# A hybrid decoder layer on one core: bias rows by the GpSimd queue, down weights as 32 KB rows, block turns by VectorE

## The chip, the cores and the metric

The kernel runs on one core of one Trainium2 chip. The metric is the device time of one launch in microseconds (us), lower is better; each number is a median over several executions.

## The reference

One inference step of one decoder layer in float32, D = 2048, for 256 prompt tokens and 8 sample tokens (one new token each for 8 sequences with a 2048-long cache). Cut to what matters:

```python
z = rms(x) @ w_in                         # 2048 x 3584: [q | k | v | u]
# 12 heads x 64: three dilated windows (128,1) (512,4) (2048,16), merged by softmax denominators,
# QK-norm, T5 relative-position bias rel_bias[bucket(distance)]
# u: 4 groups x 320 channels: causal mean over 2/4/8/16 minus the token, per-group map, scale
x = x + concat(attn, pooled) @ w_out
# cross attention, 4 heads x 128, into 256 memory tokens (prompt) or cached memory (samples)
mk, mv = rms(rms(mem) @ w_ck), rms(mem) @ w_cv
x = x + cross(rms(x) @ w_cq, mk, mv) @ w_co
# mixture of experts: top 1 of 4 groups, top 2 of its 8 experts
for e in range(32):
    y += gate * ((silu(h_e @ w_e_gate[e]) * (h_e @ w_e_up[e])) @ w_e_down[e])     # 2048x512, 2048x512, 512x2048
```

Outputs are also the new caches: the 8 sequences' key and value windows shifted by one row (about 100 MB read and written from DRAM to DRAM), the pooled state, the memory's keys and values.

## The kernel before

The program is written by hand, one instruction stream for each engine (`block.sync`, `block.gpsimd`, `block.tensor`, `block.scalar`, `block.vector`), with semaphores between them; nothing is reordered. Prompt and sample tokens are worked on together, 264 columns. Weights come through `ring`, three 4 MB slots. Slots 0 and 1 take the weight pieces of the front in turn: `CK`, `CV`, seven pieces of w_in (`IN0` to `IN0+6`), pool_w, four of w_out, `CQ`, `CO`. `big(i)` on SyncE's queue (SP) loads piece i and first waits (`piece_used`) until TensorE has used piece i-2, so each load starts at a point of TensorE's program and must land by a later one. ScalarE issues the 64 parts of the DRAM-to-DRAM cache copy (`cache_part`, 1.5 MB each) at fixed points of its own program. GpSimd's queue (POOL) loads constants, then key rows, value rows and memory rows of the samples.

PSUM is two rings of four banks: `vbank` (emptied by VectorE, order in `V_ORDER`) and `abank` (emptied by ScalarE, `A_ORDER`).

The order of TensorE's work in the front: turn the memory rows; project to memory keys (`memory_keys`); turn the x rows (16 times two 128x128 turns and a small one, L693 to L699); two small bias products and one for the row scales (L700 to L712); memory values with `CV` (L714 to L716); turn memory keys; w_in in five pieces for q, k, v (`project`, L726); in piece 1 the bias is spread: SP stores the 12 bias rows (`brow`) to DRAM, loads them back as a Hankel block, and TensorE multiplies it by a flip matrix in six products (L732 to L736) that VectorE negates into `bias`. Then ten `channels` (u) interleaved with attention scores, sample values, pool maps, `sel` (which picks each sample's own heads, L889 to L893), w_out in 16 column tiles (L895 to L913), the cross queries with `CQ`. VectorE scales the rows of `CQ` in place in four parts after the whole piece has landed (L1793 to L1797), and TensorE waits for all four (L915).

The mixture of experts: the tokens of an expert are taken in blocks of 32 (`BLK`). For each block i TensorE gathers the rows by a one-hot product (`gather`, into bank pb[0], 32 rows x 4 column quarters on the 128 partitions), ScalarE copies them out (`rows_out`), TensorE turns them (`turn_rows`), VectorE scales them by the norm gains into `XT` (`rows_in`). `expert(i)` multiplies `XT` by gate and up weights in two halves (16 rows of 512 per partition, 8 a half), ScalarE takes exp, VectorE forms `hid`, TensorE turns it, ScalarE copies it to `aT`, TensorE multiplies by the down weights, and `combine` adds the block to the tokens (VectorE, `add_results`).

On SP, `expert_weights(i)` waits for each half of expert i-1 to be used and loads the next half (2 MB of gate and 2 MB of up), then waits for the down slot and loads 4 MB:

```python
sp.dma_start(slot2.rearrange("p (k n) -> p k n", k=4), src.rearrange("(k p) n -> p k n", p=P))   # L504: 8 KB runs
```

Experts 0 and 1 are special: half 0 of expert 0 and both their down weights are loaded during the cross attention and its output; half 1 of expert 0 when `CO` has been used; the quarters of expert 1 when TensorE has used a quarter (`first_quarter`, L1153) or a half of expert 0 (L527 to L530). Before expert 0 TensorE runs filler products (`keep_busy`), the gather, and, after VectorE's `weights_of_pairs` and `blocks_over`, one small product for blocks that overflow (L1189) whose result `slots_over` turns into `over_done`, which expert 0 waits for.

Of the kernel before, what the change touches and what calls it, by code (L numbers as in the profile page):

```python
# [15 lines left out]
P = 128  # L16
# [4 lines left out]
NB = 8  # L21
# [21 lines left out]
NBUCKET, MAXD = 32, 2048  # L43
BRANCHES = ((128, 1), (512, 4), (2048, 16))
# [41 lines left out]
CONST_W = dict(ident=P, tri=P, moe=NE + NE + 3 + OVB + BLK, corr=NCORR, pools=PG * NB, flip=P, hmask=VC, sel=VG * NB,  # L86
# [9 lines left out]
def constants():  # L96
# [8 lines left out]
    part("flip")[:] = np.eye(P)[::-1]  # L105
# [26 lines left out]
V_ORDER = (["mem"] * 8 + ["gains"] + ["ck"] + ["bias"] * 2 + ["scale"] + ["cv", "in", "in"] + ["flip"] * 6 + ["in"] * 3  # L132
           + ["score"] * 12 + ["sscore"] * 2 + ["state", "svals"] + ["out"] * KT + ["cq"] * 3 + ["xscore"] * 2 + ["cq"] + ["xscore"] * 2
           + ["xsscore", "ssum", "logits", "pos"])
A_ORDER = (["ck"] + ["x"] * 16 + ["cv"] + ["mk"] * 2 + ["in", "sin"] * 5
# [12 lines left out]
def hybrid_decoder_layer(nc, a):  # L148
    with ExitStack() as ctx:
# [6 lines left out]
        bias_dram = nc.dram_tensor("bias_rows", (H, 384), F32, kind="Internal").ap()  # L156
# [41 lines left out]
        bias_flat = slot2[:, 4608:4608 + H * SEQ]  # L198
        biasS = slot2[:, 7680:7680 + NDEC]
        flip = slot2[:, 8192 - P:8192]  # L200
        hankel = qkm[:, 0:H * SEQ]
# [88 lines left out]
        XT = xfree[:, 2112:2624].rearrange("p (j s) -> p j s", j=4)  # L290
# [21 lines left out]
        w_landed = [sem("w_landed0"), sem("w_landed1")]  # L312
        v_filled, v_freed = sem("v_filled"), sem("v_freed")
# [33 lines left out]
        pick_ready, xe_filled, xe_ready = sem("pick_ready"), sem("xe_filled"), sem("xe_ready")  # L347
# [5 lines left out]
        xt_filled, xt_ready = sem("xt_filled"), sem("xt_ready")  # L353
        gate_exp, hid_seq, hid_ready = sem("gate_exp"), sem("hid_seq"), sem("hid_ready")
        hidT_filled, hidT_ready = sem("hidT_filled"), sem("hidT_ready")
# [15 lines left out]
        def piece_landed(eng, i):  # L371
            assert i != CK
            eng.wait_ge(w_landed[i % 2], 16 * (i // 2 + i % 2))
# [7 lines left out]
        N_FIRST, N_CONST = 6, 18  # L381
# [3 lines left out]
        def piece_used(eng, i):  # L385

            if i in (CK, CV):
                eng.wait_ge(v_filled, v_at(("ck", "cv")[i]))
# [22 lines left out]
        def _(sp):  # L411
            def big(i):
# [16 lines left out]
                sp.dma_start(dst, src).then_inc(w_landed[i % 2], 16)  # L429
# [10 lines left out]
            for w, lo, n in (("w_rg", 0, NG), ("w_re", NG, NE)):  # L440
# [8 lines left out]
            sp.dma_start(hankel.rearrange("p (h j) -> p h j", h=H),  # L449
                         bass.AP(tensor=bias_dram.tensor, offset=0, ap=[[1, P], [384, H], [1, SEQ]]))\  # L450
                .then_inc(bias_landed, 16)
# [65 lines left out]
            w1 = a["w_e_down"][0][1].rearrange("(k p) n -> p k n", p=P)  # L517
# [21 lines left out]
            w = a["w_e_down"][0][NE - 1].rearrange("(k p) n -> p k n", p=P)  # L539
# [22 lines left out]
        def _(pool):  # L562
# [24 lines left out]
            for dst, src in ((rb[0:NBUCKET], a["rel_bias"]), (ohp[0:33], cc("ohp", 33)), (ohs[0:33], cc("ohs", 33)),  # L587
                             (tri[:], cc("tri")), (flip, cc("flip")), (moec[:], cc("moe")), (corr[:], cc("corr")),
# [9 lines left out]
            pool.dma_start(gE[:], a["norm_ffn_g"][0].rearrange("(p k) -> p k", k=KT)).then_inc(const_landed, 16)  # L598
            pool.wait_ge(pads_ready, 1)
# [33 lines left out]
        def _(pe):  # L633
# [59 lines left out]
            for t in range(3):  # L693
                pe.wait_ge(x_landed[t], 16)
            for k in range(KT):
                bk = abank("x")
                for t in range(2):
                    turn(bk[:, P * t:P * t + P], xraw[:, t, P * k:P * k + P], ident[:])
                turn(bk[:, SEQ:TOK], xraw[0:NB, 2, P * k:P * k + P], ident[0:NB, 0:NB]).then_inc(a_filled, 1)  # L699
# [13 lines left out]

            piece_landed(pe, CV)  # L714
            project(hmT, wk(CV), 0, abank("cv"), a_filled)
# [10 lines left out]
            for n in range(5):  # L726
# [162 lines left out]
            pe.wait_ge(v_freed, v_at("svals"))  # L889
            bk = abank("sel")  # L890
            for i in range(2):
                last = mm(bk[:, 24 * i:24 * i + 24], masked[0:96, P * i:P * i + P], sel[0:96, :], start=True, stop=True)
            last.then_inc(a_filled, 1)  # L893

            for o in range(KT):  # L895
# [171 lines left out]
            all_emptied()  # L1067
# [3 lines left out]
            def gather(i):  # L1071

                pe.wait_ge(pick_ready, i + 1)
                if not (isinstance(i, int) and i == 0):
                    pe.wait_ge(xt_ready, i)
                for t in range(3):
                    n = P if t < 2 else NB
                    for c in range(4):
# [3 lines left out]

# [1031 lines left out]
```

## Time and profile before

| what | value |
|---|---|
| median of 3 runs | 1549.89 us (1549.2 to 1556.62) |
| profiled execution, its own time | 1553.96 us |
| its span (first to last instruction) | 1552.1 us |
| TensorE busy in the span | 1255.0 us, 81% |
| VectorE, ScalarE, GpSimd busy | 500.3, 194.7, 59.6 us |
| moved by the DMA engines | 608.85 MB, mean 392 GB/s |

A profile's busy time of matrix products is modelled. "PEclk" is the TensorE clock that was granted, as a share of full speed: 1.00 is 2.4 GHz, 0.50 is 1.2 GHz. "DMA share" is the mean busy share of the core's 16 DMA engines; it can read a few per cent over 1 because packets overlap. L660 is line 660 of the kernel.

### The profile page before, as it was taken

The numbers are of one execution on the slowest core, as the hardware profiler recorded it, in microseconds if no ns is written. First come the engines' busy times: TensorE is split into PE (matmuls) and PEld (weight loads), VectorE is DVE, ScalarE is ACT, GpSimd is POOL, SyncE is SP. The second block draws the span as 40 slices with busy tenths as digits, with TensorE's granted clock in tenths as the row PEclk, the third lists the DMA queues.
The fourth block names the chain that finished last, engine by engine and source line by source line (L and its number), as shares of the span: only waits on it lengthen the run. The fifth ranks groups of instructions, "written<-read, shape, count | busy, mean of one in ns | idle before, by whom it ended". The sixth has DMA issues, their size and how long they took to land.

```text
span 1552.1 us, 23601 instructions
## 1 busy us (share of the span) xinstructions
PE 1255.0 (81%) x10109; PEld 654.6 (42%) x10109; DVE 500.3 (32%) x1043; ACT 194.7 (13%) x466; POOL 59.6 (4%) x111
## 2 busy tenths in 40 slices
PE   7999999998998999877776766766776776776676
PEld 4444467765877766322222222222222222222222
DVE  2301155740103224333323323323323323332333
ACT  3200113311111233000000000000000000000000
POOL 2000022221000000000000000000000000000000
PEclk9999999999999999898989988988999899898998
DMA  9999999999999998899999999999999999999997
GB/s 352 312 375 365 356 327 391 359 319 388 383 392 350 316 409 291 336 424 425 427 427 424 429 427 423 428 427 425 427 427 425 427 427 425 426 427 426 424 428 292
DMA packets 114606, 608.85 MB, mean 392 GB/s; under 512 B 11262, under 2 KB 14485, under 8 KB 79849
## 3 DMA queue, kind: packets, MB, share of 16 engines
q1 hardware_dynamic: 72603, 479.04, 74.9%
q10 hardware_dynamic: 34550, 100.80, 17.8%
q0 software_dynamic: 7408, 28.37, 5.1%
q8 instruction: 34, 0.56, 0.1%
q14 instruction: 11, 0.09, 0.0%
HBM read 603.16 MB, written 106.18 MB: 457 GB/s over the span
## 4 chain that ended last, share of the span: by engine, by line
DMA 52%; PE 44%; DVE 2%; issue 1%; SPq 1%; ACT 0%; DVEq 0%; ACTq 0%
DMA ring<-in_w_e_up_dram 45%; PE pb L1150 11%; PE pb L660 9%; PE pb L905 6%; PE pb L746 4%; DMA ring<-in_w_out_dram 2%; DMA ring<-in_w_in_dram 2%; DMA ring<-in_w_cq_dram 2%; PE pb L1032 2%; PE pb L923 2%; PE pb L688 2%; PE pb L666 1%; SPq L490 1%; PE pb L1182 1%; PE pb L1012 1%
## 5 line engine op out<-in xcount | busy, mean ns | idle before, releaser
L1150 PE MATMUL pb<-ring,xT 128*32 128x256 f32 x4096 | 312.6, 472 | 194.0 <-DMA ring<-in_w_e_up_dram 191.5
L1150 PEld LDWEIGHTS pb<-ring,xT 128*32 128x32 f32 x4096 | 154.8, 134 | 374.9 <-DMA ring<-in_w_e_up_dram 236.1
L2033 DVE TENSOR_TENSOR Z<-pb,Z 128x512 f32<-128x512 f32 x248 | 153.7, 683 | 357.9 <-PE pb L1103 357.9
L660 PE MATMUL pb<-ring,hreg 128*128 128x512 f32 (+1 forms) x320 | 125.3, 551 | 0.0
L1182 PE MATMUL pb<-ring,xT 128*32 128x512 f32 x960 | 110.9, 603 | 0.0
L1103 PE MATMUL pb<-xT 32*128 32x512 f32 x744 | 102.9, 623 | 0.0
L1079 PE MATMUL pb<-Z,xT 128*32 128x512 f32 (+1 forms) x768 | 94.9, 608 | 0.0
L660 PEld LDWEIGHTS pb<-ring,hreg 128*128 128x128 f32 x320 | 60.3, 190 | 61.8 <-issue 60.2
L905 PE MATMUL pb<-hreg,ring 128*128 128x264 f32 x320 | 78.0, 401 | 4.7 <-DMA ring<-in_w_out_dram 4.7
L746 PE MATMUL pb<-hreg,ring 128*128 128x264 f32 x320 | 75.3, 395 | 2.1 <-DMA ring<-in_w_in_dram 2.1
L1522 ACT ACTIVATE xT<-pb 128x128 f32<-128x128 f32 x32 | 8.9, 277 | 523.0 <-PE pb L1150 523.0
L905 PEld LDWEIGHTS pb<-hreg,ring 128*128 128x128 f32 x320 | 62.2, 199 | 15.7 <-DMA ring<-in_w_out_dram 5.2
L746 PEld LDWEIGHTS pb<-hreg,ring 128*128 128x128 f32 x320 | 61.2, 193 | 14.5 <-DMA ring<-in_w_in_dram 2.5
L2030 DVE TENSOR_TENSOR Z<-pb,Z 128x512 f32<-128x512 f32 x31 | 21.4, 692 | 98.9 <-PE pb L1103 98.9
L1182 PEld LDWEIGHTS pb<-ring,xT 128*32 128x32 f32 x960 | 28.5, 111 | 55.8 <-issue 55.2
L2057 DVE TENSOR_SCALAR xT<-xT 128x128 f32<-128x128 f32 x32 | 7.3, 227 | 137.3 <-ACT xT L1522 137.3
L905 PE MATMUL pb<-Z,ring 128*128 128x264 f32 x192 | 45.3, 386 | 0.0
L1160 PE MATMUL pb<-ident,xT 128*128 128x128 f32 x32 | 10.5, 329 | 39.9 <-DVE xT L2063 39.9
L1786 DVE TENSOR_TENSOR xT<-pb,xT 128x264 f32<-128x264 f32 x16 | 6.9, 432 | 104.7 <-PE pb L905 104.7
L1087 PE MATMUL pb<-ident,xT 128*128 128x128 f32 x128 | 20.1, 280 | 25.3 <-ACT xT L1513 25.3
L1079 PEld LDWEIGHTS pb<-Z,xT 128*32 128x32 f32 (+1 forms) x768 | 18.4, 108 | 51.3 <-issue 47.5
L905 PEld LDWEIGHTS pb<-Z,ring 128*128 128x128 f32 x192 | 36.5, 190 | 6.2
(337 smaller groups left out, 1135.8 us busy)
## 6 DMA issues: line engine op xcount, KB each, us to landing
ring<-in_w_e_gate_dram SPq DMA_DIRECT2D x61, 2048.0 KB, 19.0
ring<-in_w_e_up_dram SPq DMA_DIRECT2D x61, 2048.0 KB, 23.5
ring<-in_w_e_down_dram SPq DMA_DIRECT2D x30, 4096.0 KB, 22.0
out_win_k_sample_dram<-in_cache_win_k_dram ACTq DMA_DIRECT2D x24, 1536.0 KB, 14.1
out_win_v_sample_dram<-in_cache_win_v_dram ACTq DMA_DIRECT2D x24, 1536.0 KB, 15.1
ring<-in_w_in_dram SPq DMA_DIRECT2D x7, 4096.0 KB, 29.2
ring<-in_w_out_dram SPq DMA_DIRECT2D x4, 4096.0 KB, 34.3
out_win_k_sample_dram<-in_cache_win_k_dram ACTq DMA_DIRECT2D x8, 1488.0 KB, 15.8
```

Of the source, the lines that this page charges most:

```text
L660: last = mm(bk[:, 0:n], xt[:, k, tile * P:tile * P + P], w[:, k, 0:n], start=(k == 0), stop=(k == KT - 1))
L688: last = mm(bk[:, :], hmT[:, k, tile * P:tile * P + P], wk(CK)[:, k, :], start=(k == 0), stop=(k == KT - 1))
L746: last = mm(bk[:, 0:TOK], w[:, k, :], hT[:, k, :], start=(k == 0), stop=(k == KT - 1))
L905: last = mm(bk[:, 0:TOK], w[:, k, :], mix(k), start=(i == 0), stop=(i == KT - 1))
L923: last = mm(bk[:, 0:TOK], wk(CQ)[:, k, XD * h:XD * h + XD], xT[:, k, :], start=(k == 0), stop=(k == KT - 1))
L1032: last = mm(pb[o % 4][:, 0:TOK], wo[:, h, P * o:P * o + P], oT[:, h, :], start=(h == 0), stop=(h == XH - 1))
L1079: last = mm(pb[0][32 * c:32 * c + 32, :], pick[0:n, t, :], xn[0:n, t, 512 * c:512 * c + 512], start=(t == 0), stop=(t == 2))
L1103: last = mm(out, GT[r, cols], yo[r, :], start=True, stop=True)
L1150: last = mm(pb[1][32 * c:32 * c + 32, 0:256], XT[:, k % 4, 32 * (k // 4):32 * (k // 4) + 32], w[:, :, k8, P * c:P * c + P], start=(k == 0) ...
L1182: last = mm(pb[3][32 * c:32 * c + 32, :], aT[:, 32 * f:32 * f + 32], w[f][:, 512 * c:512 * c + 512], start=(f == 0), stop=(f == 3))
L2030: last = V.tensor_tensor(x3s, banks[0][:, :], x3s, ALU.add)
L2033: last = V.tensor_tensor(d, banks[c][:, :], d, ALU.add)
```

## The change

- **Bias.** The Hankel block, the flip matrix and its six products go. VectorE negates the 12 bias rows; GpSimd's queue stores them 32 times over in DRAM (590 KB), waits, and loads the bias already flipped in four DMAs with a row step of 383 elements. SP no longer waits for any of it. ScalarE waits for the store ahead of the turned queries and keys, VectorE for the loads ahead of the first scores.
- **Order of the memory part.** The bias and scale products come right after the memory keys; the x turns are interleaved, one for each of the 16 steps of the first memory-value product; both memory-value tiles are emptied by VectorE. Two cache parts move from w_in's piece 1 to the x turns.
- **sel.** `choose_heads` moves into w_out's first tile, ahead of its 10th step (k = 15).
- **CQ** comes in four DMAs with a semaphore each; VectorE scales a quarter after each of the last four w_out tiles, and the first cross query waits for a quarter every fourth step.
- **Down weights.** Partition p takes rows 4p to 4p+3, so one 32 KB run for each partition in place of four of 8 KB. (Expert 1's in two DMAs of 16 KB runs; the last expert's four quarters keep 4 KB runs.)
- **Block turns.** VectorE turns 32x32 blocks: the gathered rows straight from PSUM, and `hid`. TensorE's `turn_rows`, its turn of `hid` and ScalarE's two copies go. `turn_gates` moves ahead of the wait for `hid`. ScalarE's `rows_back` copies become plain.
- **First block.** `rows_in(0)` comes ahead of `weights_of_pairs`; the overflow product moves behind the first half of expert 0, to its own bank; ten filler products stand between the first gather and expert 0.

```diff
-            sp.wait_ge(v_freed, v_at("bias", 0))
-            sp.dma_start(bias_dram[:, :], brow[0:H, :]).then_inc(brow_stored, 16)
-            sp.wait_ge(brow_stored, 16)
-            sp.wait_ge(v_freed, v_at("bias", 1))
-            sp.dma_start(hankel.rearrange("p (h j) -> p h j", h=H), ...).then_inc(bias_landed, 16)
...
+            pool.wait_ge(v_freed, v_at("bias", 0))
+            pool.dma_start(bias_dram[:, :, :], brow[0:H, :].unsqueeze(1).to_broadcast([H, REPS, 384])).then_inc(brow_stored, 16)
+            pool.wait_ge(brow_stored, 16)
+            for r in range(0, P, REPS):
+                pool.dma_start(bias[r:r + REPS],
+                               bass.AP(tensor=bias_dram.tensor, offset=P - 1 - r, ap=[[384 - 1, REPS], [384 * REPS, H], [1, SEQ]]))\
+                    .then_inc(bias_landed, 16)
...
-            project(hmT, wk(CV), 0, abank("cv"), a_filled)
+            cv0 = vbank("cv")
+            for k in range(KT):
+                last = mm(cv0[:, :], hmT[:, k, 0:P], wk(CV)[:, k, :], start=(k == 0), stop=(k == KT - 1))
...
+                turn(bk[:, SEQ:TOK], xraw[0:NB, 2, P * k:P * k + P], ident[0:NB, 0:NB]).then_inc(a_filled, 1)
...
-                if n == 1:
-                    pe.wait_ge(bias_landed, 16)
-                    for f in range(6):
-                        mm(vbank("flip")[:, :], flip, hankel[:, 512 * f:512 * f + 512], start=True, stop=True)\
-                            .then_inc(v_filled, 1)
...
+                    if o == 0 and k == KT - 1:
+                        choose_heads()
...
+                if i == CQ:
+                    for j in range(4):
+                        sp.dma_start(dst[:, 4 * j:4 * j + 4], src[:, 4 * j:4 * j + 4]).then_inc(cq_landed[j], 16)
...
-            pe.wait_ge(wq_scaled, 4)
+                    if h == 0 and k % 4 == 0:
+                        pe.wait_ge(wq_scaled, k // 4 + 1)
...
-                if o in (KT - 3, KT - 2):
-                    piece_landed(dve, CQ)
+                if o >= KT - 4:
+                    k = 4 * (o - KT + 4)
+                    dve.wait_ge(cq_landed[o - KT + 4], 16)
...
-                sp.dma_start(slot2.rearrange("p (k n) -> p k n", k=4), src.rearrange("(k p) n -> p k n", p=P))\
+                sp.dma_start(slot2, src.rearrange("(p k) n -> p (k n)", k=4))\
...
             def rows_in(i):
-                dve.wait_ge(xt_filled, i + 1)
-                V.tensor_tensor(XT.rearrange(...), pb[0][:, :].rearrange(...), gE[:]..., ALU.mult).then_inc(xt_ready, 1)
+                dve.wait_ge(xe_filled, i + 1)
+                V.transpose(xe.rearrange("p (k s) -> p k s", k=KT), pb[0][:, :].rearrange("p (q k) -> p k q", k=KT))\
+                    .then_inc(xe_turned, 1)
+                dve.wait_ge(xe_turned, i + 1)
+                V.tensor_tensor(XT, xe.rearrange("p (k s) -> p k s", k=KT), gE[:].unsqueeze(2).to_broadcast([P, KT, BLK]),
...
-                pe.wait_ge(hid_ready, i + 1)
-                nc.tensor.transpose(pb[2][:, 0:P], hid, ident[:]).then_inc(hidT_filled, 1)
...
+                dve.wait_ge(hid_ready, i + 1)
+                V.transpose(aT.rearrange("p (f s) -> p f s", f=4), hid.rearrange("p (q f) -> p f q", f=4)).then_inc(hidT_ready, 1)
...
             gather(0)
-            turn_rows(0)
-            pe.wait_ge(over_cols_ready, 1)
-            mm(pb[1][:, 0:NE], ones[0:NE, :], over_cols, start=True, stop=True).then_inc(over_filled, 1)
-            pe.wait_ge(over_done, 1)
+            keep_busy(10)
             expert(0)
...
             choose(0)
+            rows_in(0)
             weights_of_pairs()
             blocks_over()
-            rows_in(0)
             slots_over()
```

## Rows read from the trace of the kernel before

**Rows 1.** The page's chain that ended last, by engine

```profile
DMA 52%; PE 44%; DVE 2%; issue 1%; SPq 1%; ACT 0%; DVEq 0%; ACTq 0%
```

**Rows 2.** Stretches: us, busy PE, PEld, DVE, ACT, POOL; PEclk, DMA share, GB/s

```profile
100.00:150.00 50.00, 50.00 (x337) 25.18 (x326) 2.25 (x4) 2.64 (x9) 0.00 (x0) 1.00 1.03 380
...
400.00:450.00 50.00, 50.00 (x239) 42.65 (x238) 5.42 (x14) 7.06 (x14) 5.76 (x8) 1.00 1.00 384
...
800.00:1000.00 200.00, 142.05 (x1487) 55.35 (x1487) 64.09 (x134) 14.34 (x34) 0.00 (x0) 0.91 1.01 426
```

**Rows 3.** SP queue's packets, MB, share in 1084:1090.5, 30:35, and one block 800:829.5

```profile
q1 hardware_dynamic: 332, 2.72, 100.4%
...
q1 hardware_dynamic: 66, 2.16, 100.4%
...
q1 hardware_dynamic: 1104, 12.58, 100.9%
```

**Rows 4.** Chain that ended last, in order of time: start, us, what

```profile
55.19 29.45 PE pb L660 x64
...
102.86 27.66 PE pb L660 x64
...
148.07 5.15 PE pb L735 x12
```

**Rows 5.** A stretch behind the x turns, columns as in rows 2

```profile
52.00:55.00 3.00, 3.00 (x9) 1.83 (x8) 1.14 (x3) 0.63 (x1) 0.00 (x0) 0.50 1.00 365
```

**Rows 6.** Landing of w_in: IN0, then all seven (second row: min, median, max)

```profile
ring<-in_w_in_dram SPq DMA_DIRECT2D x1, 4096.0 KB, 24.7
...
DMA to landing us min/median/max: 19.0/29.2/38.7
```

**Rows 7.** Timeline of TensorE at the start of w_out

```profile
365.88 1.01 PE L892 MATMUL pb<-sel,s_in 96*128 96x24 f32 x4 [0.61 <-DVE s_in L1772]
368.37 6.88 PE L905 MATMUL pb<-hreg,ring 128*128 128x264 f32 x20 [1.48 <-DMA ring<-in_w_out_dram]
```

**Rows 8.** Timeline around the landing of CQ, VectorE and TensorE

```profile
493.16 4.49 DVE L1797 TENSOR_TENSOR ring<-ring,gT 128x2048 f32<-128x2048 f32 x2 [10.79 <-DMA ring<-in_w_cq_dram]
496.51 0.60 PE L912 MATMUL pb<-ident,qkm 128*128 128x128 f32 x4
...
502.80 16.03 PE L923 MATMUL pb<-xT,ring 128*128 128x264 f32 x64 [5.68 <-DVE ring L1797]
```

**Rows 9.** Landing of CK's first and third quarter, issued together

```profile
ring<-in_w_ck_dram SPq DMA_DIRECT2D x1, 1024.0 KB, 11.0
...
ring<-in_w_ck_dram SPq DMA_DIRECT2D x1, 1024.0 KB, 17.9
```

**Rows 10.** Timeline, all engines, from the routing to expert 1

```profile
611.82 2.20 PE L1057 MATMUL pb<-ident 128*128 128x128 f32 x18
...
613.95 2.91 PE L1079 MATMUL pb<-Z,xT 128*32 128x512 f32 x24
...
618.48 0.67 DVE L2023 TENSOR_TENSOR xT<-pb,gE 128x512 f32<-128x512 f32 x1
...
619.80 9.84 PE L1150 MATMUL pb<-ring,xT 128*32 128x256 f32 x128 [0.56 <-DVEq L1981]
...
623.50 0.33 SPq L499 DMA_DIRECT2D ring<-in_w_e_gate_dram  x1
...
643.60 3.64 PE L1150 MATMUL pb<-ring,xT 128*32 128x256 f32 x64
...
647.46 0.35 SPq L490 DMA_DIRECT2D ring<-in_w_e_gate_dram  x1
```

**Rows 11.** Two stretches of 4 us there, columns as in rows 2

```profile
620.00:624.00 4.00, 4.00 (x40) 1.77 (x36) 3.47 (x14) 0.00 (x0) 0.00 (x0) 0.50 0.04 14
644.00:648.00 4.00, 4.00 (x68) 2.00 (x60) 0.00 (x0) 0.43 (x1) 0.00 (x0) 1.00 0.25 98
```

**Rows 12.** Chain that ended last, the last expert: start, us, what

```profile
1533.93 0.30 DVE xT L2063
...
1534.27 0.34 PE pb L1160
...
1535.55 3.58 PE pb L1129 x22
```

More of the change, by code:

```diff
@@ L43 @@
 NBUCKET, MAXD = 32, 2048
+REPS = 32
 BRANCHES = ((128, 1), (512, 4), (2048, 16))
@@ L84 @@
 NCORR = sum(n for _, _, n in CORR)
-CONST_W = dict(ident=P, tri=P, moe=NE + NE + 3 + OVB + BLK, corr=NCORR, pools=PG * NB, flip=P, hmask=VC, sel=VG * NB,
+CONST_W = dict(ident=P, tri=P, moe=NE + NE + 3 + OVB + BLK, corr=NCORR, pools=PG * NB, hmask=VC, sel=VG * NB,
                ohp=384, ohs=NDEC)
@@ L128, in constants @@
     return c
-V_ORDER = (["mem"] * 8 + ["gains"] + ["ck"] + ["bias"] * 2 + ["scale"] + ["cv", "in", "in"] + ["flip"] * 6 + ["in"] * 3
+V_ORDER = (["mem"] * 8 + ["gains"] + ["ck"] + ["bias"] * 2 + ["scale"] + ["cv"] * 2 + ["in"] * 5
            + ["score"] * 12 + ["sscore"] * 2 + ["state", "svals"] + ["out"] * KT + ["cq"] * 3 + ["xscore"] * 2 + ["cq"] + ["xscore"] * 2
            + ["xsscore", "ssum", "logits", "pos"])
-A_ORDER = (["ck"] + ["x"] * 16 + ["cv"] + ["mk"] * 2 + ["in", "sin"] * 5
+A_ORDER = (["ck"] + ["x"] * 16 + ["mk"] * 2 + ["in", "sin"] * 5
            + ["u"] + ["qk"] * 6 + ["u", "u"] + ["turn"] * 2 + ["u", "uout", "val"] + ["turn"] * 2
@@ L312, in hybrid_decoder_layer @@
         w_landed = [sem("w_landed0"), sem("w_landed1")]
+        cq_landed = [sem(f"cq_landed{i}") for i in range(4)]
         v_filled, v_freed = sem("v_filled"), sem("v_freed")
@@ L371, in piece_landed @@
         def piece_landed(eng, i):
-            assert i != CK
+            assert i not in (CK, CQ)
             eng.wait_ge(w_landed[i % 2], 16 * (i // 2 + i % 2))
@@ L712, in _ @@
             last.then_inc(v_filled, 1)
+            for t in range(3):
+                pe.wait_ge(x_landed[t], 16)
             piece_landed(pe, CV)
-            project(hmT, wk(CV), 0, abank("cv"), a_filled)
+            cv0 = vbank("cv")
+            for k in range(KT):
+                last = mm(cv0[:, :], hmT[:, k, 0:P], wk(CV)[:, k, :], start=(k == 0), stop=(k == KT - 1))
+                if k == KT - 1:
+                    last.then_inc(v_filled, 1)
+                bk = abank("x")
+                for t in range(2):
+                    turn(bk[:, P * t:P * t + P], xraw[:, t, P * k:P * k + P], ident[:])
+                turn(bk[:, SEQ:TOK], xraw[0:NB, 2, P * k:P * k + P], ident[0:NB, 0:NB]).then_inc(a_filled, 1)
             project(hmT, wk(CV), 1, vbank("cv"), v_filled)
@@ L888, in _, with choose_heads @@
             assert kt == UT
[L889 to L893, printed above, removed]
+            def choose_heads():
+                pe.wait_ge(v_freed, v_at("svals"))
+                bk = abank("sel")
+                for i in range(2):
+                    last = mm(bk[:, 24 * i:24 * i + 24], masked[0:96, P * i:P * i + P], sel[0:96, :], start=True, stop=True)
+                last.then_inc(a_filled, 1)
             for o in range(KT):
@@ L1074, in gather @@
                 if not (isinstance(i, int) and i == 0):
-                    pe.wait_ge(xt_ready, i)
+                    pe.wait_ge(xe_turned, i)
                 for t in range(3):
                     n = P if t < 2 else NB
+                    if t == 1 and not (isinstance(i, int) and i < 2):
+                        pe.wait_ge(y_added, 3 * i - 4)
                     for c in range(4):
@@ L1081, in gather @@
                 last.then_inc(xe_filled, 1)
-            def turn_rows(i):
-                pe.wait_ge(xe_ready, i + 1)
-                for j in range(4):
-                    last = nc.tensor.transpose(pb[0][:, P * j:P * j + P], xe[:, P * j:P * j + P], ident[:])
-                last.then_inc(xt_filled, 1)
             def turn_gates(i):
@@ L1154, in expert @@
                     last.then_inc(gu_used[half], 1)
+                    if first and half == 0:
+                        pe.wait_ge(over_cols_ready, 1)
+                        pe.wait_ge(v_freed, nv)
+                        mm(pb[3][:, 0:NE], ones[0:NE, :], over_cols, start=True, stop=True).then_inc(over_filled, 1)
                     if not first:
@@ L1163, in expert @@
                     if not first:
-                        pe.wait_ge(y_added, 3 * i - 1)
-                    turn_rows(i + 1)
-                    if not first:
                         combine_in_turn(i, 2)
+                if not first:
+                    pe.wait_ge(gt_ready, i)
+                turn_gates(i)
                 pe.wait_ge(hidT_ready, i + 1)
-                turn_gates(i)
                 if last_of_all:
@@ L1641, in _ @@
                 head_norm(mk, t, P, XH, XD, msq, gck, mk_normed)
-            freed(V.tensor_scalar(mv[:, 1, :], filled("cv")[:, :], st[:, 22:23], None, ALU.mult))
+            for t in range(2):
+                freed(V.tensor_scalar(mv[:, t, :], filled("cv")[:, :], st[:, 21 + t:22 + t], None, ALU.mult))
             dve.wait_ge(v_freed, nv)
-            dve.wait_ge(a_freed, a_at("cv"))
             dve.nop().then_inc(mk_normed, 1)
@@ L1657, in sample_scores @@
                                 AX.X, ALU.add).then_inc(keys_used, 1)
-            for n in range(2):
+            for n in range(3):
                 project(n)
-            for f in range(6):
-                freed(V.tensor_scalar(bias_flat[:, 512 * f:512 * f + 512], filled("flip")[:, :], -1.0, None, ALU.mult))
-            project(2)
             dve.wait_ge(v_freed, nv)
```

74 lines of the change are left out of this document (26 added, 48 removed).

## The prediction

> **What bounds the kernel now.** First the chain that ended last: transfers hold 52% of it, TensorE 44%, the rest 4% [rows 1]. Which of them holds where is read from the stretches. In w_in and w_out (100 to 150, 400 to 450) TensorE is busy all the time and the DMA share is about 1 too [rows 2]: TensorE sets the pace, since SP issues each load when TensorE has used a slot, but the transfers have next to no room. In the experts (800 to 1000) TensorE is busy 71% and the transfers 1.01 at 426 GB/s [rows 2]: there the bytes set the end, and a faster block saves nothing. So the change has three places: TensorE's time before expert 0, the gaps in the transfers around experts 0 and 1, and the speed at which weights flow after that.
>
> **How fast weights flow.** The packet view is read at three moments when SP's queue is alone. The first is all down weights, 8 KB packets: 332 packets in 6.5 us at 100.4% of 16 engines, so 1.004 x 6.5 x 16 / 332 = 0.3145 us each. The second is the load of CV, which has 32 KB for each partition in one run: 66 packets of 2.16 MB in 5 us at 100.4%, 1.217 us each. The third is one block, 1104 packets, of which 1024 carry data (512 of 8 KB, 512 of 16 KB; five transfers end with 16 small ones each) [rows 3]. Four 8 KB packets take 1.258 us, one of 32 KB takes 1.217: 0.041 us less, about 14 ns for each packet saved. An engine moves 32 small packets of a down load in 10.06 us, or 8 large ones in 9.74: 0.325 us for each expert. The loads that change in the stretch where transfers never pause are those of experts 2 to 30, 29 of them: **9.4 us**. The low bound is nothing, if the packets' times overlap with something that stays; against it speaks that shares of 1.00 go with both sizes.
>
> A page's rule gives less. The Trainium skill, DMA: Bandwidth & Descriptors, section Why small descriptors are slow, charges a fixed 3 cycles beside one cycle for each 32 bytes: by it 8 KB is 259 cycles and 32 KB 1027, so my estimate from the page is 0.9% of a down load in place of the 3.2% of the rows, some 2.5 us in all in place of 9.4; the trace disagrees on the size, and I go by the trace.
>
> **The front, part by part.** *Flip products.* They hold the chain for 5.15 us inside w_in [rows 4]; nothing else runs on TensorE then, and their wait for the bias goes with them: **5.15 us**. The bias by GpSimd's queue costs TensorE nothing: it is issued near 46 and needed only when scores begin near 250 (VectorE waits there, with the samples' scores behind it); the key rows behind it on that queue wait until about 200 anyway. SP loses two transfers and two waits, which IN0+1 stood behind but did not suffer from: its slot came free only when TensorE had used CV, near 84.7 (55.19 + 29.45) [rows 4].
>
> *Order of the memory part.* TensorE's work is the same. But behind 8 us of turns the granted clock is 0.50, its lower level of 1.2 GHz [rows 5], and the memory values took 29.45 us where as many products take 27.66 later [rows 4]; the small bias and scale products run there too. Interleaved with products of full size the turns should not pull the clock down: 1.8 us, and some 0.7 of the small products. **2.5 us**, from 0 (the clock falls all the same) to 3.7. VectorE's chain gets later: the last x row arrives near 68 instead of 52, then 6.6 us of scaled rows and 6.2 of key norms end near 81.3, when TensorE, near 81.5, wants the normed keys (both added up from the same program's steps as the trace has them). That is level; a microsecond late would be a microsecond lost.
>
> *Does the DMA keep up?* w_in's loads land in 19 to 38.7 us, median 29.2 [rows 6], and TensorE needs 31.3 for a piece (27.66 for two tiles [rows 4] and 3.6 for the samples): 2 us of room. IN0 (24.7) [rows 6] will meet the bias on GpSimd's queue (2.1 MB with the 32-fold store) and two more copy parts; issued at 47.8 and needed near 82 it has 34. The work only moves, but 0.59 MB is new: 1.5 us at 390 GB/s. I take **-2 us** for late landings, between 0 and -8.
>
> *sel.* It ended 1.5 us before w_out's first piece landed [rows 7], so moving it behind that landing puts its 1.01 us (0.5 at full clock) on the path: **-0.5**, between -1 and +1 (if w_out lands earlier).
>
> *CQ.* The piece landed at 493.16, VectorE then scaled 9 us, and TensorE, done with w_out at 497.1, stood 5.68 us [rows 8]. Four DMAs issued together land one after another, as CK's quarters did (first 11.0, third 17.9 us) [rows 9], so three are scaled while w_out still runs, and the fourth (2.3 us, behind the sum of tile 15) is ready near 500, while the first cross query wants it 5.3 us after 497. **5.7 us**, low bound 0 if all four land late, because VectorE waits in order and tile sums stand behind it.
>
> **Around experts 0 and 1.** The gather ends at 616.86, then come ScalarE's copy, the turn, the scaling (618.48) and the overflow product, and expert 0 starts at 619.80 [rows 10]. Now VectorE turns and scales. Its turn isn't in the trace; the nearest row of that shape is 0.67 us (618.48), one with a stride from PSUM may take 2; so `XT` is ready between 618.4 and 619.8. TensorE meanwhile does ten fillers: 18 records took 2.20 us [rows 10], so 20 take 2.44, and expert 0 starts at 619.3, 0.5 us earlier. More comes from the clock: it was 0.50 from 620 to 624 [rows 11], so the first quarter took 3.7 us (to SP's issue at 623.50) where a full-speed half is 3.64 [rows 10]. The fillers leave no pause, so a quarter should take 1.8, and SP issues at 621.2. The transfers stand still in two gaps here: share 0.04 from 620 to 624 and 0.25 from 644 to 648 [rows 11], 6.8 us together. The first shrinks by 2.3. The second ends with SP's issue at 647.46, when half 0 of expert 1 is used; expert 1 started at 643.60 [rows 10] behind hid's turn, the second gather, copy, turn and the down product. The gather no longer waits for `hid`, but VectorE now does `slots_over` and the second choice later, so it starts near 630 instead of 632.2: the second gap shrinks by about 2.2. **4.5 us**, from 0.5 to 6.8.
>
> **The tail.** From the end of `hid` (1534.23) to the last down product (1535.55) stand a turn, a copy and the gates' turn, 1.32 us [rows 12]. One turn by VectorE, like the 0.30 of the row before it, remains: **0.9 us**, from 0 to 1.1. In the other blocks all this is hidden by the transfers; `XT` was ready some 7 us before its weights, so a slow turn costs nothing there until it takes that long.
>
> **The sum.** 9.4 + 5.15 + 2.5 - 2 - 0.5 + 5.7 + 4.5 + 0.9 = 25.65 us. The profiled execution took 1553.96 us (span 1552.1 and 1.9 around it): 1528.3. It was 4.07 us over the median of the runs shown, so on the median's scale 1549.89 - 25.65 = **1524.2 us**.
>
> **Rivals.** *The packets matter less than that* (15 in 100): the flow is bounded by what all 16 engines share, the large packets wait longer in turn, and the loop stays at 426 GB/s. Then 9.4 goes: 1533.6. For it: both sizes read a share of 1.00, and a busy share may hold waiting; against it: a line through the two sizes (14 ns and 37.6 ns for each KB) gives 0.615 us for 16 KB, and with that the block, 512 x (0.3145 + 0.615) / 16 = 29.75 us, which is the row's 1.009 x 29.5 [rows 3]. The page's three cycles are this rival at its mildest, 1531.1.
>
> *The transfers take the front's gain back* (16 in 100). The share is 1.03 from 100 to 150 and 1.00 from 400 to 450 [rows 2]; if copies pushed out of their places make w_in and w_out land later, the flips, the clock and part of CQ's wait come back as waits for weights: 8 us less, 1532.2.
>
> *The front's loads fall behind* (4 in 100), which ends slower. A landing of 38.7 us was seen, with key rows on a third queue [rows 6]. If GpSimd's bias and the copies brought that to IN0 to IN0+3, IN0 would come 4.5 us late and each of the next three 7.4 us past TensorE's 31.3: 26.6 us, more than the gain, 1550.8. From 38.5 us for a load it decides; the median load of 29.2, with two queues busy, speaks against it.
>
> The forecast, all parts about as summed, has 65 in 100 (its own range 1518 to 1530). Above and below it the bounds reach 1517 (both gaps closed, the clock whole) and 1538 (no packet gain and 5 us of the front lost): **1517 to 1538** holds 8 in 10. A measurement here can tell 0.5%, 7.7 us, from no change; so faster (below 1542.1) 0.94, same 0.03, slower 0.03.
>
> **What would show it.** In the packet view of a block 640 packets with data instead of 1024, about 1.217 us for those of 32 KB, and a period of blocks 0.33 us shorter (12.58 MB at 426 GB/s are 29.5). In the chain no flip products, memory values at 27.7 to 28 us with the turns taken out, no wait for CQ between w_out and the cross queries. No stretch with a share near 0.04 between the gather and expert 1. Wrong it would be with waits for w_in or w_out of more than 5 us in all, with a period still at 29.5, or if VectorE's turn took over 2 us and expert 0 waited for it.

## The result, and the profile after

The changed kernel takes 1541.44 us (median of 7 runs) beside 1553.58 for the kernel before on the same chip: a ratio of 0.9937, 95% interval 0.9919 to 0.9955, so 7 to 12.6 us faster. The ratio is that of the fast runs; one of the seven, at a lower granted clock, took 1609.19 us and is left out of it. Forecast were 1524.2 us and a range from 1517 to 1538: the sign is right, the size is not. The profiled execution took 1539.83 us (span 1538.0), 14.1 us under the profiled one of before; the sum had 25.65. So 11.5 us are missing, and the two traces say where.

The page's chain by engine, then the three stretches (columns as in [rows 2]), and a fourth, from 90 to 95:

```profile
DMA 49%; PE 46%; DVE 2%; issue 2%; SPq 1%; ACT 0%; DVEq 0%; ACTq 0%
```

```profile
100.00:150.00 50.00, 50.00 (x356) 25.34 (x355) 0.69 (x1) 3.23 (x10) 0.00 (x0) 1.00 1.03 382
400.00:450.00 50.00, 50.00 (x239) 42.78 (x238) 4.80 (x13) 6.09 (x13) 4.33 (x6) 1.00 1.00 383
800.00:1000.00 200.00, 149.51 (x1449) 50.95 (x1453) 74.46 (x153) 8.07 (x21) 0.00 (x0) 0.82 1.01 430
```

```profile
90.00:95.00 5.00, 2.56 (x3) 1.17 (x4) 0.00 (x0) 0.00 (x0) 0.00 (x0) 0.50 1.04 409
```

The bounds are those of [rows 1, 2]; in the experts the transfers move 430 GB/s in place of 426. TensorE's granted clock there fell from 0.91 to 0.82, which costs nothing while the transfers set the pace. Next the chain of the changed kernel through the front (start, us, what), and under it three pieces of the kernel before, which [rows 4] doesn't hold:

```profile
69.16 13.93 PE pb L662 x32
83.09 0.87 PE pb L727 x8
83.96 8.48 issue
92.44 16.53 PE pb L662 x32
108.97 3.61 PE pb L668 x128
...
220.37 36.82 DMA ring<-in_w_in_dram
```

```profile
85.52 13.73 PE pb L660 x32
...
215.80 35.62 DMA ring<-in_w_in_dram
251.46 7.39 PE pb L746 x32
```

The flip products are gone, and the memory values run at full clock (13.93 for the second tile). But at 83.96 TensorE stands for 8.48 us. The trace names no releaser ("issue"); what comes next are the products of IN0, and IN0 is still on its way. Behind the pause the first 32 product records take 16.53 us where they take 13.73 to 13.95 elsewhere; the granted clock is 0.50 from 90 to 95. So the pause costs 11.1 us. It comes back in the two runs below whose program is the same up to here: 9.14 us with CQ as before, 9.18 without the fillers. SP's and GpSimd's DMA issues, and the packets of two queues from 48 to 52 (packets, MB, share of 16 engines), show why IN0 is late:

```profile
43.88 8.34 SPq L444 DMA_DIRECT2D b<-in_b_re_dram  x1
52.27 31.22 SPq L431 DMA_DIRECT2D ring<-in_w_in_dram  x2
...
45.56 0.70 POOL L595 DMA_DIRECT2D bias_rows<-qkm  x1 [35.20 <-DVE qkm L1621]
55.38 2.48 POOL L598 DMA_DIRECT2D ring<-bias_rows  x4 [9.12 <-DMA bias_rows<-qkm]
```

```profile
q0 software_dynamic: 70, 0.27, 52.7%
q1 hardware_dynamic: 150, 0.02, 18.6%
```

GpSimd's 32-fold store of the bias (0.59 MB) is issued at 45.56 (0.70 us) and lands 9.1 us after that. While it runs, SP's queue (q1) moves only 150 packets in 4 us, small ones of the router's weights and b_re, and SP can't finish issuing b_re: 8.34 us in place of 3.66. IN0, behind it, is issued at 52.27 in place of 47.84, and its landing takes 40.1 us in place of 24.7 [rows 6]: 92.4. At w_out TensorE is still 5 us behind the kernel before, for all the flips it no longer does:

| start of | before | changed | store 8-fold (last run below) |
|---|---|---|---|
| IN0's products | 85.52 | 92.44 | 83.71 |
| issue of IN0+5 | 215.80 | 220.37 | 210.03 |
| IN0+5's products | 251.46 | 257.23 | 245.37 |
| w_out | 368.37 | 373.58 | 362.32 |
| first cross query | 502.80 | 501.81 | 491.42 |
| expert 0 | 619.80 | 616.52 | 606.13 |
| expert 1 | 643.78 | 635.58 | 625.07 |
| span | 1552.1 | 1538.0 | 1527.4 |

CQ's wait [rows 8] is gone: the cross queries follow the last product of w_out at once (chain).

```profile
494.25 7.12 PE pb L910 x32
501.38 0.44 PE pb L917 x4
501.81 14.24 PE pb L928 x64
```

The first 64 of them take 14.24 us, not 16.03 [rows 8]: the old pause had slowed them too. Around experts 0 and 1, the timeline of the turn, then the chain, then three stretches of 4 us:

```profile
614.16 0.72 DVE L2010 STREAM_TRANSPOSE xT<-pb 128x512 f32<-128x512 f32 x1 [1.95 <-PE pb L1087]
614.91 0.69 DVE L2013 TENSOR_TENSOR xT<-xT,gE 128x512 f32<-128x512 f32 x1
```

```profile
614.09 2.43 PE pb L1062 x20
616.52 3.59 PE pb L1151 x64
...
627.15 4.34 PE pb L1087 x24
...
635.58 3.45 PE pb L1151 x64
```

```profile
616.00:620.00 4.00, 4.00 (x69) 2.31 (x67) 2.70 (x15) 0.00 (x0) 0.00 (x0) 1.00 0.39 117
620.00:624.00 4.00, 4.00 (x70) 2.27 (x66) 3.03 (x12) 0.00 (x0) 0.00 (x0) 1.00 0.94 387
636.00:640.00 4.00, 4.00 (x66) 1.87 (x56) 0.00 (x0) 0.23 (x1) 0.00 (x0) 1.00 0.95 395
```

VectorE's turn, strided from PSUM, takes 0.72 us and hides behind the fillers; expert 0 runs at full clock; of the two gaps [rows 11] one remains, at 0.39. Expert 1 starts 19.06 us after expert 0, before 23.98. That the edits closed the second gap is not shown by this: the first experiment, which has none of them, has no second gap either. The packets of one block, of 8 us with 32 KB packets alone (101 and two small ones) and of 14 us with 16 KB packets (363 and 41 small ones):

```profile
q1 hardware_dynamic: 720, 12.58, 100.5%
...
q1 hardware_dynamic: 103, 3.31, 96.1%
...
q1 hardware_dynamic: 404, 5.95, 99.8%
```

640 packets carry data (80 are small). 0.961 x 8 x 16 / 101 = 1.217 us for 32 KB, as forecast, and 0.998 x 14 x 16 / 363 = 0.616 for 16 KB. Yet the period of blocks is 29.294 us (26 of them, from 692.68 to 1454.32) and before it was 29.520: 0.226 less, not 0.325. The tail, last expert in the chain, 0.48 us from the end of `hid` (1520.82) to the last down product, where 1.32 were [rows 12]:

```profile
1520.51 0.30 DVE xT L2052
...
1520.84 0.42 DVE xT L2054
...
1521.30 3.65 PE pb L1130 x22
```

### The profile page after: what moved, and what is told of

It reads as the page before. It is cut to its first block, busy times and chain, and to the rows that moved or that the text cites. A ratio compares the mean times of both kernels' runs of the same rounds, so it can differ in the third digit from the quotient of the medians.

```text
span 1538.0 us, 23238 instructions
## 1 busy us (share of the span) xinstructions
PE 1279.9 (83%) x9957; PEld 632.7 (41%) x9957; DVE 531.9 (35%) x1102; ACT 167.0 (11%) x401; POOL 62.6 (4%) x115
## 4 chain that ended last, share of the span: by engine, by line
DMA 49%; PE 46%; DVE 2%; issue 2%; SPq 1%; ACT 0%; DVEq 0%; ACTq 0%
DMA ring<-in_w_e_up_dram 42%; PE pb L1151 12%; PE pb L662 8%; PE pb L910 6%; DMA ring<-in_w_out_dram 5%; PE pb L746 4%; DMA ring<-in_w_in_dram 2%; PE pb L1037 2%; PE pb L928 2%; PE pb L690 2%; PE pb L714 1%; PE pb L1185 1%; PE pb L668 1%; PE pb L1087 1%; SPq L485 1%
## 5 line engine op out<-in xcount | busy, mean ns | idle before, releaser
L1151 PE MATMUL pb<-ring,xT 128*32 128x256 f32 x4096 | 288.1, 443 | 121.2 <-DMA ring<-in_w_e_up_dram 115.9
L1151 PEld LDWEIGHTS pb<-ring,xT 128*32 128x32 f32 x4096 | 144.1, 127 | 285.3 <-DMA ring<-in_w_e_up_dram 153.7
L1087 PE MATMUL pb<-Z,xT 128*32 128x512 f32 (+1 forms) x768 | 135.1, 797 | 95.2 <-DVE Z L2022 92.1
L1104 PE MATMUL pb<-xT 32*128 32x512 f32 x744 | 169.2, 750 | 0.0
L1185 PE MATMUL pb<-ring,xT 128*32 128x512 f32 x960 | 137.9, 726 | 0.0
L662 PEld LDWEIGHTS pb<-ring,hreg 128*128 128x128 f32 x320 | 61.2, 193 | 72.2 <-issue 70.5
L1185 PEld LDWEIGHTS pb<-ring,xT 128*32 128x32 f32 x960 | 32.4, 131 | 79.0 <-issue 78.3
L1104 PEld LDWEIGHTS pb<-xT 32*128 32x128 f32 x744 | 30.4, 153 | 66.5 <-issue 66.5
L1518 ACT COPY xT<-pb 128x264 f32<-128x264 f32 x32 | 12.2, 380 | 314.1 <-PE pb L1096 314.1
L1639 DVE COPY Z<-pb 128x512 f32<-128x512 f32 (+1 forms) x5 | 3.2, 638 | 112.5 <-PE pb L662 112.5
## 6 DMA issues: line engine op xcount, KB each, us to landing
ring<-in_w_out_dram SPq DMA_DIRECT2D x4, 4096.0 KB, 34.9
```

The source lines that it names most:

```text
L662: last = mm(bk[:, 0:n], xt[:, k, tile * P:tile * P + P], w[:, k, 0:n], start=(k == 0), stop=(k == KT - 1))
L1087: last = mm(pb[0][32 * c:32 * c + 32, :], pick[0:n, t, :], xn[0:n, t, 512 * c:512 * c + 512], start=(t == 0), stop=(t == 2))
L1104: last = mm(out, GT[r, cols], yo[r, :], start=True, stop=True)
L1151: last = mm(pb[1][32 * c:32 * c + 32, 0:256], XT[:, k, :], w[:, :, k8, P * c:P * c + P], start=(k == 0), stop=(k == KT - 1))
L1185: last = mm(pb[3][32 * c:32 * c + 32, :], aT[:, 32 * f:32 * f + 32], w[f][:, 512 * c:512 * c + 512], start=(f == 0), stop=(f == 3))
```

## The experiments

Theory: the front lost its gain because the bias store holds IN0 up, and the packets gave less because their durations overlap. Rivals: it is the late issue alone, the cache copies, or the bytes of the front as a whole; the new order of work eats a part of the packets' gain. Ratios are to the kernel before, timed on the same chip. The runs of one kernel spread over 7 to 16 us here, so spans and marks of one profiled execution each stand beside them. A mark has a spread too: two executions with the same front, the changed kernel's and that without fillers, end the first gather 2.5 us apart (614.09 and 616.64).

| run | ratio (95%) | IN0 issued + landing | expert 0 | span |
|---|---|---|---|---|
| changed | 0.9937 (0.9919 to 0.9955) | 52.3 + 40.1 = 92.4 | 616.5 | 1538.0 |
| 32 KB rows alone | 0.9969 (0.9949 to 0.9989) | | | 1543.1 |
| copies moved | 0.9952 (0.9933 to 0.9971) | 52.0 + 24.8 = 76.8 | 619.0 | 1546.9 |
| bias behind IN0 | 0.9874 (0.9842 to 0.9906) | 48.3 + 23.2 = 71.5 | 610.4 | 1532.6 |
| both | 0.9951 (0.9931 to 0.9971) | 47.3 + 14.1 = 61.4 | 618.2 | 1543.1 |
| reads behind IN0 | 0.9905 (0.9871 to 0.9939) | 52.1 + 35.0 = 87.1 | 615.4 | 1540.3 |
| bias behind IN0+2 | 0.9907 (0.9881 to 0.9934) | 48.5 + 23.7 = 72.2 | 617.1 | 1538.9 |
| CQ whole | 0.9994 (0.9973 to 1.0015) | | 627.3 | 1549.2 |
| no fillers | 0.9939 (0.9916 to 0.9963) | | 618.2 | 1542.6 |
| IN0 ahead of b_re | 0.9928 (0.9905 to 0.9952) | 44.4 + 44.3 = 88.7 | 617.2 | 1538.4 |
| that, bias behind IN0 | 0.9886 (0.9867 to 0.9906) | 43.7 + 22.1 = 65.8 | 612.3 | 1536.4 |
| no copies | 0.9760 (0.9740 to 0.9781) | 42.0 + 24.4 = 66.4 | 589.1 | 1511.1 |
| store 8-fold | 0.9893 (0.9876 to 0.9909) | 48.6 + 34.9 = 83.5 | 606.1 | 1527.4 |

**32 KB rows alone, in the kernel before.**

```diff
-sp.dma_start(slot2.rearrange("p (k n) -> p k n", k=4), src.rearrange("(k p) n -> p k n", p=P))
+sp.dma_start(slot2, src.rearrange("(p k) n -> p (k n)", k=4))
```

> The kernel before with one edit: the down weights of experts 0 and 2 to 30 are loaded as one 32 KB row for each partition (hid keeps its old order, so the sums pair other rows; the work is the same). Theory: the changed kernel's blocks are 0.22 us shorter (29.29 against 29.51) and that is all that the packets give, because packets overlap a little (the share is above 1) and fewer packets overlap less: 29 x 0.22 = 6.4 us faster than before, blocks of 29.29. Rival 1: the packets give the 0.325 us that was predicted, and the changed kernel loses a third of it by its new order of work: 9.4 us faster here, blocks of 29.18. Rival 2: the shorter block comes from the new order and not from the packets: no change here, blocks of 29.51.

Blocks of 29.29 us, as in the changed kernel; the chain, one block:

```profile
921.05 6.53 PE pb L1150 x64
...
950.34 5.39 PE pb L1150 x64
```

The ratio means 2 to 8 us less. The theory's 6.4 lies inside, the predicted 9.4 does not, nor does nothing. The packets alone make the shorter block. The profiled execution gives 9.0 us (span 1543.1), but only some 6 of them lie in the blocks. The rest comes ahead of them: this run starts expert 0 as the kernel before does (619.74), and yet the second gap [rows 11] isn't there. TensorE's clock differed, first the kernel before, then this run, from 632 to 636; the third line is this run where the gap had been:

```profile
632.00:636.00 4.00, 4.00 (x21) 0.83 (x25) 0.00 (x0) 0.27 (x1) 0.00 (x0) 0.57 1.02 430
```

```profile
632.00:636.00 4.00, 3.29 (x31) 1.11 (x27) 0.67 (x1) 0.88 (x2) 0.00 (x0) 1.00 1.02 424
...
644.00:648.00 4.00, 2.87 (x56) 1.52 (x52) 3.80 (x9) 0.00 (x0) 0.00 (x0) 1.00 1.00 408
```

The second half of expert 3, which waits for its weights in all three kernels, starts 80.6 us after expert 0 in the kernel before, 76.8 here and 76.2 in the changed kernel. The gather and the down product ahead of expert 1 took 4.58 and 5.34 us in the kernel before and 2.92 and 3.64 here. So nearly all that the changed kernel wins around experts 0 and 1 is won here too, without its edits there.

**Copies moved.**

```diff
 freed(copy(xT[:, k, :], filled("x")[:, 0:TOK]))
-if k % 4 == 3:
-    cache_part()
...
-cache_part((2, 1, 2, 1, 0)[n])
+cache_part((2, 1, 3, 2, 0)[n])
...
-cache_part((2, 2, 2, 1, 1)[n])
+cache_part((2, 2, 2, 2, 2)[n])
```

> The changed kernel, with the four parts of the cache copy that ScalarE issues among the x turns moved to w_in's pieces 2, 3 and 4. Theory: IN0 landed at 92.4 because copies and bias share the engines with it (14.4 MB moved in the 40 us it took, 4.2 of them IN0); without 6.3 MB of copies it lands near 77, TensorE no longer stands 8.5 us, and the clock no longer drops behind the pause (16.53 back to 13.93): 11 us faster than the changed kernel's 1541.4, so 1530. Rival 1: the late issue (52.3 in place of 47.8) is what matters: IN0 still lands past 84 and less than half of the 11 us comes. Rival 2: all bytes of the front bound it together: the pause goes, but waits for w_in and w_out grow by as much, 1541.

IN0 landed at 76.8 as the theory had it, TensorE didn't stand for it, and nothing was won: IN0+5 now took 45.2 us to land, TensorE stood 11.6 us for it, and expert 0 started later than in the changed kernel. The second rival holds for the place to which the copies went.

**Bias behind IN0.**

```diff
 pool.wait_ge(v_freed, v_at("bias", 0))
+piece_landed(pool, IN0)
 pool.dma_start(bias_dram[:, :, :], ...)
```

> The changed kernel, with GpSimd waiting for IN0's landing before it stores and reads the bias. Theory of the late issue: the bias store holds up the issue of b_re (8.3 us in place of 3.7), so IN0 is issued at 47.8 again, 4.5 us earlier, and with the bias' 1.8 MB away (some 4.6 us at 390 GB/s) it lands near 83.5: nearly all of the 11 us, 1531. Theory of the copies alone: IN0 gains only the 4.6 us of the bytes, lands near 88, and TensorE still stands some 4 us and is slowed behind it: 1537. Rival: the bias read later meets w_in's pieces, and the gain is lost there: 1541.

b_re's issue took 3.98 us, IN0 was issued at 48.3 and landed 23.2 us later, earlier than either theory said. The bias then met IN0+1 (35.4 us; TensorE stood 3.3 and ran its next 32 records in 16.76). Expert 0 starts 6.1 us earlier than in the changed kernel.

**Both edits.**

> The changed kernel with both edits of the two runs before. Either alone may already be enough to land IN0 before TensorE wants it (84.0); then both together give no more than the better of them, 1530. If the sum of bytes in the front sets the end, both together give 1541 as well. If each removes a part of the wait, this run is the fastest of the three.

IN0 landed at 61.4, and it was no use: the copies were back at IN0+5 (44.1 us, a wait of 10.5). Of the three expectations only the second, that the bytes set the end, fits.

**Reads behind IN0, the store where it was.**

```diff
 pool.wait_ge(brow_stored, 16)
+piece_landed(pool, IN0)
 for r in range(0, P, REPS):
```

> The changed kernel, with only the four bias reads (1.57 MB) held back until IN0 has landed; the 32-fold store of the bias stays where it is. If the store does the harm, by holding up the issue of b_re and of IN0 behind it (52.3 in place of 47.8), IN0 is still issued near 52 and lands some 4 us before 92.4 (1.57 MB at 390 GB/s), near 88: TensorE still stands about 4 us and runs slowed behind that, and the time lies halfway, near 1537 to 1538. If the reads do the harm, TensorE no longer stands and the time is that of the run with all of the bias held back, some 1534.

The store's case: b_re's issue 8.29 us, IN0 at 52.1, landed at 87.1, a pause of 4.1 us. The ratio lies halfway, but the interval of these four runs holds both ends. By the landing, 5.3 us earlier than in the changed kernel, the reads carry a part of it.

**Bias behind IN0+2.**

```diff
 pool.wait_ge(v_freed, v_at("bias", 0))
+piece_landed(pool, IN0 + 2)
```

> The changed kernel, with GpSimd storing and reading the bias only when IN0+2 has landed. With the bias behind IN0 alone, it met IN0+1: TensorE stood 3.3 us for that and ran the next product sum 2.8 us slower. Behind IN0+2 the trace of the changed kernel has a share of 0.9 from 140 to 180, so there is room: if the bias' bytes are all there is to it, both waits go, IN0+5 is issued near 208.5 and the end comes some 6 us earlier than with the bias behind IN0, near 1528. Rival: the front's bytes then bind at IN0+5 as they did with the copies moved (a landing of 45 us), and this run is no faster than 1534.

The rival: IN0 and IN0+1 came in time, but TensorE then stood 4.2 us for IN0+2 and 6.2 for a later piece of w_in (47.2 us from issue to use). Expert 0 starts 6.7 us later than with the bias behind IN0; timed, the two places can't be told apart, since their intervals overlap.

**CQ as before.** One DMA, scaling in two halves, one wait ahead of the cross queries.

```diff
-for j in range(4):
-    sp.dma_start(dst[:, 4 * j:4 * j + 4], src[:, 4 * j:4 * j + 4]).then_inc(cq_landed[j], 16)
+sp.dma_start(dst, src).then_inc(cq_landed[0], 16)
```

> The changed kernel with CQ loaded, scaled and waited for as before: one DMA, VectorE's scaling in two halves behind tiles 13 and 14, one wait ahead of the cross queries. If the 5.7 us were really on the path, TensorE stands 5 to 6 us ahead of the first cross query; and if the slow clock behind the pause belongs to it (the first 64 cross-query products took 16.03 us before and 14.24 after), expert 0 starts 7 to 7.5 us later than 616.5, and the kernel takes 7 us more, 1548. Rival: what the front gives is taken back at the experts' first transfers, and the end moves by less than 3 us.

```profile
460.15 7.14 PE pb L909 x32
...
467.30 32.96 DMA ring<-in_w_cq_dram
...
507.58 2.30 DVE ring L1783
...
510.01 16.87 PE pb L927 x64
```

Even more than expected: the queries start 8.2 us later and run 2.6 slower, expert 0 starts 10.8 us later, and the ratio is 1 within its interval. CQ's load itself was issued 1.0 us later than in the changed kernel (467.30 and 466.31), which the edit can't have done; some 9.8 us are left. So in the changed kernel the CQ edit carries more than the whole gain of the front, 3.3 us at expert 0.

**No fillers behind the first gather.**

```diff
 gather(0)
-keep_busy(10)
 expert(0)
```

> The changed kernel without the ten filler products behind the first gather. Prediction's reason: without them TensorE pauses for the copy-free turn by VectorE, the granted clock falls to 0.50, expert 0's first quarter takes 3.7 in place of 1.8 us, SP issues the next weights some 2 us later, and since transfers set the end from there on, the kernel takes 1.5 to 2.5 us more. Rival: the pause is too short for the clock to fall, expert 0 starts at the same time or a little earlier, and the end doesn't move.

```profile
616.66 0.73 DVE xT L2009
...
618.16 5.35 PE pb L1151 x64
```

The clock does fall: the 64 records take 5.35 us in place of 3.59. But they start sooner behind the gather, and the half is done 6.9 us after the gather's end in place of 6.0. Timing can't tell this from the changed kernel; whether more than the 0.9 us reaches the end stays open.

**IN0 ahead of b_re.** The two statements change places.

> The changed kernel, with SP issuing IN0 ahead of b_re (16 KB in rows of 128 B, spread to all partitions) in place of behind it; the bias stays where it is. If the place behind b_re is what makes IN0 late, IN0 is issued near 44 and its bytes flow 8 us earlier: it lands near 84 to 85 in place of 92.4, TensorE stands 1 us or not at all, and the time is at most 1534 (as with the bias held back), a little less if IN0+1, which then doesn't meet the bias, lands without a wait. If the bias store chokes all queues (72 to 138 GB/s from 48 to 56 in the changed kernel), IN0 gains little by it: it lands past 88, and the time is 1537 or more.

The place isn't it: now IN0's own issue takes 7.67 us, it lands at 88.7, and TensorE stands 6.5.

**IN0 ahead of b_re, bias behind IN0.**

> The changed kernel with both: IN0 ahead of b_re, and the bias held back until IN0 has landed. IN0 then lands near 68, the bias is done some 4 us earlier than with the bias held back alone (reads near 78 in place of 82) and meets IN0+1 for less time: TensorE's 3.3 us wait for IN0+1 shrinks, at best 6 us are won with the clock behind it, 1528 to 1534. Rival: the bytes of w_in bind from IN0+1 on, and the time stays at 1534.

IN0 landed at 65.8, but IN0+1 and IN0+2 still cost 4.1 us of waiting: no better than the bias behind IN0 alone.

**No cache copies.** The counters run on, the DMAs are left out.

> The changed kernel without the copy of the cache windows from DRAM to DRAM (64 parts of 1.5 MB and less, so the cache outputs are left out). It shows how much of TensorE's waiting in the front is competition with copies. If the front is bound by bytes wherever TensorE waits for weights, IN0's pause (8.5), IN0+5's wait (3.3) and w_out's (5.8) all go, with the slow clock behind them, and expert 0 starts 20 us or more earlier than 616.5; the kernel takes 1520 or less. If only IN0's place in the queues is wrong, the pause stays at 4 us or more and the rest stays as well.

Expert 0 starts 27.4 us earlier. No wait for w_in is left, and 0.5 us for w_out. So none of TensorE's waits for weights in the front is there without the copies; for IN0's pause other edits did as much.

**Store 8-fold.**

```diff
-REPS = 32
+REPS = 8
```

> The changed kernel with the bias stored 8-fold (144 KB) in place of 32-fold (576 KB), and read back by 16 DMAs of 8 rows in place of 4 of 32. If the store chokes the queues (9.5 us of it at 45.6), it now takes some 3 us, b_re's issue takes 4 us in place of 8.3, IN0 is issued near 48 and lands near 84 to 86: TensorE stands 2 us or less, 1534 to 1536. If the reads' bytes or the copies are what counts, IN0 lands past 89, and the time is above 1537.

The store lands in 4.8 us, b_re's issue takes 4.16, and up to IN0's products the chain is what had been forecast:

```profile
82.83 0.87 PE pb L727 x8
83.71 13.79 PE pb L662 x32
97.50 3.61 PE pb L668 x128
```

Expert 0 starts 10.4 us earlier than in the changed kernel and 13.7 earlier than before; the span is 24.7 us under that of before. From 52 to 56 the transfers move 364 GB/s where the changed kernel's moved 138. Timed, the gain over the changed kernel is smaller (0.9893, an interval clear of 0.9937's), some 7 us; the profiled execution was the fastest of the five. It and the two runs with the bias behind IN0 and the copies in their place are the best versions; their intervals overlap.

## Why the prediction was wrong, step by step

The median missed the forecast by 17.2 us. Of these, 3.7 are the base, 1549.89 as the median of three runs against 1553.58 of seven; the rest is gain that didn't come. Against the profiled executions, in us saved:

| step | forecast | measured | from |
|---|---|---|---|
| down packets | 9.4 | 6.5 | 29 x (29.520 - 29.294) |
| flips | 5.15 | 5.0 | IN0 to IN0+5's issue 130.28, then 127.93, and 2.6 of slow clock in it |
| memory part | 2.5 | 1.6 | 85.52 to 83.96 |
| late landings | -2 | -12.3 | 8.48 and 2.6 at IN0, 1.2 at IN0+5 |
| sel | -0.5 | 0.6 | IN0+5 to w_out 116.91, then 116.35 |
| rest of w_out | 0 | 0.5 | to its fourth piece 96.58, then 96.06 |
| CQ | 5.7 | 5.7 | fourth piece to the queries 37.85, then 32.17 |
| cross part, start of expert 0 | 0.5 | 2.3 | 117.00, then 114.71 |
| gaps around experts 0 and 1 | 4 | 3.4 | what remains of 14.1; not shown to come from the edits |
| tail | 0.9 | 0.8 | 1.32, then 0.48 |

**The step that failed is "Does the DMA keep up?"** It priced the bias by bytes: "0.59 MB is new: 1.5 us at 390 GB/s", and took -2 us for all late landings, at worst -8; measured are -12.3. That store took 9.1 us for its 0.59 MB, and its price was not its own time but what stood behind it: b_re's issue, IN0's issue, IN0's bytes, TensorE, and TensorE's clock. The run with the store 8-fold shows it: a quarter of the store, and 10.4 us are back at expert 0. IN0 is issued 3.7 us earlier there, and its landing is 5.2 us shorter (34.9); the issue alone is not enough, since IN0 issued at 44.4 beside the full store still landed at 88.7. It is not the whole of IN0's landing: without the copies, store and all, IN0 landed at 66.4, and with the bias held back and the copies moved at 61.4. The four copies, the whole bias or three quarters of the store: any one of them taken away brings IN0 in time, and the store is the one whose removal costs least later. The rival "the transfers take the front's gain back" had late landings and nearly the size (8 us), but put them down to the copies alone and not to the store; it got 16 in 100, as the room was judged by IN0's landing of before (24.7 of 34), and that row had been taken with the engines free of this store.

**The packets were mis-sized by a third.** The durations were right (1.217 and 0.616 us), but an engine's time is not the wall's: the packets of a block add up to 29.74 us an engine before and 29.42 after (0.615 for 16 KB), while the blocks last 29.52 and 29.29. The rest, 0.22 and 0.13 us, is overlap between neighbours, some 3 ns a packet in both. So 384 packets fewer save 0.325 us of engine time and lose 0.1 of overlap. The share of 1.009 [rows 3] said so; the forecast used it to check the row and not to correct the saving. The Trainium skill, DMA: Bandwidth & Descriptors, section Why small descriptors are slow, charges three cycles a packet, from which the forecast's estimate of 2.5 us was worked out. The trace doesn't agree on the size: in the run of the rows alone the blocks are 0.23 us shorter, 6.7 us over 29.

**Right** were the flips, CQ, the tail and the cheap turn by VectorE. Of the gaps the first shrank, and expert 0 ran at full clock, as forecast. The second closed too, but its length before hung on the clock in that one execution, and it is gone in the run of the rows alone: that 4 became 3.4 is luck in part. The row of sel is not sel's own time: its four products, 0.36 us, lie inside w_out's first tile now, and w_out landed 0.6 us sooner after its issue. VectorE's normed keys came at 82.6, level with TensorE, as the forecast feared. Not counted was that each pause has a second price: the products behind it run slowed. It raised CQ's worth by 1.8 us and IN0's loss by 2.6. Of the bounds, 1517 doesn't follow from the two terms named beside it: the rest of the gaps (2.3) and of the clock (1.2) give 1520.7.

## What to carry to other kernels

Price a small transfer by what its queue neighbours do while it runs, not by bytes at full rate: a store of 0.6 MB cost 10 us at expert 0 here, because the weights wanted next were issued later and landed more slowly beside it. Where copies and weights fill the DMA engines, a copy put off can come back at the next tight piece, as the four did here at IN0+5; no run here found a place where they cost nothing. Before a gap between transfers is written into a sum, look whether a second execution has it. From a share above 1, take the overlap off before multiplying a saving per packet by their number.

## What the runs showed of the hardware

The 192 packets of the 32-fold store (3 KB each, from 12 partitions) took 0.335 us each (40.2% of 16 engines from 45 to 55), and 0.21 where it ran later, as the bias behind IN0; the 64 of the 8-fold store (2.3 KB each) took 0.10 (7.5% from 45 to 50.2). An 8 KB packet of weights takes 0.3145 [rows 3]. With the 32-fold store running, SP's queue moved 150 packets from 48 to 52; with the bias held back 1001 packets under 512 B went in the same 4 us, with the store 8-fold 846. The kernel before, with no store but with cache copies beside it, moved 474 there. Why the store holds the other queue up, no run here isolates.
